# A two-block kernel on one core: first-norm statistics in the load stage, a bias read backwards, and first down weights split ahead

## The reference, cut to what matters

```
mod = silu(c) @ w_mod + b_mod;  sh1, sc1, g1, sh2, sc2, g2 = split(mod, 6)
h = rms(x, norm1_w) * (1 + sc1) + sh1
u, q, k, v = split(h @ w_in)             # 512, 512, 128, 128 columns
y_ssm  = z * sigmoid(z @ w_glu + b_glu), z = gelu(state space model of u)
y_attn = attention(rms(q), rms(k), v)    # window 128, logits + bias[bucket(distance)], a sink
x = x + g1 * (concat(rms(y_ssm), rms(y_attn)) @ w_out)
h2 = rms(x, norm2_w) * (1 + sc2) + sh2
val, gate = split(conv3(h2 @ w_up) + conv_b)
x = x + g2 * ((silu(gate) * val) @ w_down)         # inner width 2816
```

## Time and profile before

| | us |
|---|---|
| median of 3 executions (lowest, highest) | 2991.18 (2987.18, 2992.55) |
| the profiled execution, its own time | 2984.72 |
| its span, first to last instruction | 2982.9 |
| TensorE busy in the span | 2592.6 (87%) |
| VectorE busy | 1635.1 (55%) |
| ScalarE busy | 954.5 (32%) |
| mean granted TensorE clock | 0.931 of full |

### The profile page before, as it was taken

The page is one execution under the profiler, slowest core; times in us unless marked ns, Lnnn a source line. Parts: engine busy times, 40 slices in busy tenths (PEclk is TensorE's granted clock), DMA queues, the critical chain, the costliest instruction groups (busy, mean ns, idle before and its releaser), DMA issues. The chain is left out here.

```text
span 2982.9 us, 39459 instructions
## 1 busy us (share of the span) xinstructions
PE 2592.6 (87%) x16795; PEld 1389.9 (47%) x16795; DVE 1635.1 (55%) x2092; ACT 954.5 (32%) x1082; POOL 35.6 (1%) x66
## 2 busy tenths in 40 slices
PE   5988585899999989998785878897887999998997
PEld 2446463344444434443453657576332444443443
DVE  4767744654454443435205766668566677775243
ACT  3315204542332321313015454444343222222131
POOL 0010000010000000000000000000000000000000
PEclk7999798899999999999877989998999999999999
DMA  7125364212212113322010000000210112122433
GB/s 262 50 64 185 100 214 142 57 29 56 56 42 56 53 51 108 96 67 78 4 36 22 13 24 22 15 15 1 71 29 15 53 45 56 42 56 63 125 98 95
DMA packets 299447, 198.99 MB, mean 67 GB/s; under 512 B 11281, under 2 KB 294063, under 8 KB 298800
## 3 DMA queue, kind: packets, MB, share of 16 engines
q1 hardware_dynamic: 298438, 196.70, 22.2%
q10 hardware_dynamic: 873, 0.32, 0.0%
HBM read 187.02 MB, written 9.45 MB: 66 GB/s over the span
## 5 line engine op out<-in xcount | busy, mean ns | idle before, releaser
L199 PE MATMUL ps<-hT,arena 128*128 128x512 bf16 (+1 forms) x6384 | 1389.0, 380 | 80.5 <-DVE arena L238 24.2
L199 PEld LDWEIGHTS ps<-hT,arena 128*128 128x128 bf16 x6384 | 626.7, 99 | 831.3 <-issue 62.1
L199 PE MATMUL ps<-arena 128*128 128x512 bf16 x2112 | 462.5, 382 | 28.1 <-DVE arena L1781 28.1
L199 PEld LDWEIGHTS ps<-arena 128*128 128x128 bf16 x2112 | 207.8, 98 | 281.5 <-issue 37.6
L2022 DVE SCALAR_TENSOR_TENSOR arena<-ps,vec,arena 128x945 f32<-128x945 f32 (+2 forms) x176 | 215.1, 1222 | 79.2 <-ACT arena L2008 59.8
L1989 DVE SCALAR_TENSOR_TENSOR arena<-ps,vec,arena 128x1023 f32<-128x1023 f32 (+1 forms) x88 | 106.7, 1275 | 185.0 <-ACT arena L1979 185.0
L1781 DVE TENSOR_TENSOR arena<-hT,arena 128x2816 bf16<-128x2816 f32 x32 | 98.9, 3092 | 147.0 <-ACT arena L1777 146.9
L2614 PE MATMUL ps<-arena 128*128 128x128 f32 x896 | 125.8, 301 | 55.6 <-DVE arena L2884 46.6
L1777 ACT ACTIVATE arena<-hT 128x2816 bf16<-128x2816 f32 x32 | 81.6, 2550 | 283.0 <-DMA hT<-w_down_dram 106.8
L2614 PEld LDWEIGHTS ps<-arena 128*128 128x128 f32 x896 | 119.5, 214 | 62.5 <-DVE arena L2884 49.5
L1936 DVE TENSOR_TENSOR arena<-hT,arena 128x2048 bf16<-128x2048 f32 x44 | 100.9, 2292 | 35.7 <-ACT arena L1903 35.7
(11 more groups left out here) (405 smaller groups left out, 2594.8 us busy)
## 6 DMA issues: line engine op xcount, KB each, us to landing
xT<-ada_w_dram SPq DMA_DIRECT2D x24, 1024.0 KB, 6.4
hT<-w_up_dram SPq DMA_DIRECT2D x44, 512.0 KB, 5.0
hT<-w_down_dram SPq DMA_DIRECT2D x32, 704.0 KB, 6.7
hT<-ffn_up_dram SPq DMA_DIRECT2D x44, 512.0 KB, 4.9
hT<-ffn_down_dram SPq DMA_DIRECT2D x32, 704.0 KB, 7.0
arena<-w_in_dram SPq DMA_DIRECT2D x35, 512.0 KB, 4.1
xT<-w_mod_dram SPq DMA_DIRECT2D x16, 1024.0 KB, 5.2
arena<-w_mod_dram SPq DMA_DIRECT2D x8, 1024.0 KB, 19.1
```

What stands on the lines that cost most here:

```text
L199: last = pe.matmul(out, lhs(a, kt), rhs(b, kt, i), start=start and kt == 0 and (a, b) == (0, 0), stop=stop and kt == n_k - 1 and (a, b) == ...
```

## The change

1. **Statistics early.** `norm1` is made in stage_load. ScalarE squares the tiles as they are copied; TensorE sums half 0 by eight products with ones into bank 6 (no additions), half 1 goes by VectorE's additions and one product as before; Ln and Exp of both halves follow in pairs (`act_roots`). stage_project starts with the scaling. The root sits in `masks`.
2. **Mirrored bias.** The rows are copied reversed, so the windows land with the right partition and reversed columns, straight in `bias`; attention reads them with step -1. The flip, its product and its copy leave. The three small products stand behind the first `exact_half`.
3. **Loads.** The first three exact weights are loaded in stage_load; in stage_project the save of x, the other weights and two of the stream are issued ahead of the bias's round trip.
4. **x back.** Its load moves from the end of stage_ssm into stage_glu, behind two weights.
5. **First down weights.** Unit 0's are loaded once the last up weights are split and split in three pieces: rows 0 to 15, 16 to 20, and the last row at a place of its own. Even units keep two regions, odd ones another. TensorE makes rows 0 to 20 of units 0 and 1, then the last row of both, whose g is finished last.
6. **Later sums.** The sum in unit 9 stands ahead of row 18.

```diff
@@ stage_load: sync, scalar, tensor, vector
+            sp.wait_ge(turned, n_units + 1)
+            for n in range(3):
+                weights, source = exact_weights(k, n)
+                sp.dma_start(weights, source).then_inc(k.exact_in[n], 16)
...
+            def squares(first, end):
+                for i, n, a, b, t in norm.steps()[first:end]:
+                    act.wait_ge(copied, i + 1)
+                    if i >= 4:
+                        act.wait_ge(square_used if i < KD + 4 else norm.used, i - 3)
+                    act.activation(norm.sq[:, i % 4, :], k.xT[:, t, a:b], ACT.Square).then_inc(norm.sqd, 1)
+            squares(0, KD)
             act.wait_ge(copied, n_units + 2)
...
             act.activation(p_exp, p_exp, ACT.Exp).then_inc(exped, 1)
+            squares(KD, 2 * KD)
+            norm.act_roots(act)
...
+            pe.wait_ge(copied, n_units - 3)
+            square_sums(range(0, 4))
             pe.wait_ge(rows_in, 16 * len(loads))
...
             last.then_inc(turned, 1)
+            square_sums(range(4, KD))
+            pe.sem_inc(norm.summed, 1)
             pe.wait_ge(silu_c, 1)
...
+                if i == 5:
+                    norm.pe_sums(pe, (1,))
...
+            dve.wait_ge(norm.summed, 1)
+            dve.sem_inc(norm.used, KD)
+            norm.dve_stats(dve, (1,))
@@ stage_project: sync, scalar, vector
+            sp.dma_start(k.x_kept, k.xT[:, :, :]).then_inc(k.x_saved, 16)
...
-                        window = bass.AP(k.rows_dram, (4 * g + 2 * t + j) * RB, [[1, P], [1, 2 * WINDOW]])
-                        sp.dma_start(mirrored[:, 4 * g + 2 * j + t, :], window).then_inc(fetched, 16)
+                        window = bass.AP(k.rows_dram, (4 * g + 2 * t + j) * RB + 1, [[1, P], [1, 2 * WINDOW]])
+                        sp.dma_start(bias[:, 4 * g + 2 * j + t, :], window).then_inc(fetched, 16)
...
-            norm.act_squares(act)
-            norm.act_finish(act)
+            norm.act_affine(act)
...
-            norm.dve_centre(dve)
+            norm.dve_gain(dve)
+            norm.dve_finish(dve)
...
-            dve.tensor_copy(rows[0:N_Q, :], k.ps[0:N_Q, 6, 0:RB]).then_inc(copied, 1)
+            dve.tensor_copy(rows[0:N_Q, :], k.ps[0:N_Q, 7, P:P + RB][:, ::-1]).then_inc(copied, 1)
@@ stage_attention, stage_ssm, stage_glu
-                link(dve.scalar_tensor_tensor(x, src, scale, bias[:, g, :, 2 * WINDOW - nk:2 * WINDOW], ALU.mult, ALU.add))
+                link(dve.scalar_tensor_tensor(x, src, scale, bias[:, g, :, 0:nk][:, :, ::-1], ALU.mult, ALU.add))
...
-            sp.wait_ge(w_ready, 1)
-            sp.dma_start(k.xT[:, :, :], k.x_kept).then_inc(k.x_back, 16)
...
                 stream.load(sp, n)
+                if n == 1:
+                    sp.dma_start(k.xT[:, :, :], k.x_kept).then_inc(k.x_back, 16)
@@ DownByHalves, Ffn
+    def first_hi(self, act, f):
+        act.wait_ge(self.first_loaded, 32)
+        act.wait_ge(f.made[0], FT // 2 + 1)
+        for i, (raw, parts) in enumerate(self.first_splits()):
+            if i == 1:
+                act.wait_ge(f.done[0], FT // 2 + 1)
+            act.activation(parts[:, 0], raw, ACT.Copy).then_inc(self.first_hi_done, 1)
...
+    def first_units(self, pe, f):
+        pe.wait_ge(self.first_lo_done, 1)
+        self.span(pe, 0, 0, self.FIRST)
+        pe.wait_ge(self.first_lo_done, 2)
+        self.span(pe, 0, self.FIRST, FT - 1).then_inc(self.rows_done, 1)
+        pe.wait_ge(self.lo, 1)
+        self.span(pe, 1, 0, FT - 1)
+        pe.wait_ge(self.first_lo_done, 3)
+        pe.wait_ge(f.done[1], FT // 2 + 1)
+        for u in range(2):
+            self.span(pe, u, FT - 1, FT).then_inc(self.made, 1)
...
+        sp.wait_ge(self.lo[1], FT // 2 + 1)
+        down.load_first(sp)
         for b in range(2):
             sp.wait_ge(self.made[b], FT // 2 + 1)
...
         self.act_unit(act, FT // 2 - 1, 0)
-        self.act_unit(act, FT // 2 - 1, 1, down_hi)
+        down.first_hi(act, self)
+        self.act_unit(act, FT // 2 - 1, 1, lambda: down.split_hi(act, 1))
...
-                    if u == KD + 1 and kt == 6:
+                    if u == KD + 1 and kt == 18:
                         m_norm.pe_sums(pe, (0,))
```

More of the change, by code:

```diff
@@ L279, in stage_load @@
     p_exp, p_sum = (k.ar(M_BLOCKS + 2 * KD * 32 + 2 * HG_HEADS * i, 2 * HG_HEADS) for i in range(2))
+    k.norm1 = norm = norm1(k)
+    square_used = k.sem("square_used")
+    k.exact_in = [k.sem(f"exact_in{n}") for n in range(QK_TILES)]
     x_in = [k.sem(f"x_in{g}") for g in range(2)]
@@ L1781, in split_lo, with part @@
-        dve.tensor_tensor(self.parts(u, 1), self.raw, self.parts(u, 0), ALU.subtract).then_inc(self.lo, 1)
+        dve.wait_ge(self.hi, u)
+        for raw, parts in self.splits(u):
+            last = dve.tensor_tensor(parts[1], raw, parts[0], ALU.subtract)
+        last.then_inc(self.lo, 1)
+    def part(self, u, s, kt):
+        if u % 2:
+            return self.w_odd[:, s, kt, :]
+        if (u, kt) == (0, FT - 1):
+            return self.last_row[:, s, 0, :]
+        i = kt >= self.FIRST
+        return self.w_even[i][:, s, kt - self.FIRST * i, :]
@@ new lines, in span @@
+    def span(self, pe, u, first, end, before=None):
+        cols = slice((u // KD) * HALF, (u // KD + 1) * HALF)
+        for kt in range(first, end):
+            if before is not None:
+                before(kt)
+            for a, b in PASSES:
+                last = pe.matmul(self.bank(u), self.part(u, a, kt), self.g[:, b, kt, cols],
+                                 start=kt == 0 and (a, b) == (0, 0), stop=kt == FT - 1 and (a, b) == PASSES[-1],
+                                 skip_group_check=True)
+        return last
@@ L1785, in unit @@
[L1785 removed]
+        pe.wait_ge(self.lo, u)
         if u >= 4:
             pe.wait_ge(self.read, u + 1 - (4 if u < KD else self.second_banks))
[L1788 to L1790 removed]
+        self.span(pe, u, 0, FT, before).then_inc(self.made, 1)
     def bank(self, u):
@@ L2202, in _ @@
             act.wait_ge(ctx_saved, 16)
-            f.act(act, lambda: down.split_hi(act, 0))
-            act.wait_ge(f.done[0], FT // 2 + 1)
-            for u in range(1, 2 * KD):
+            f.act(act, down)
+            for u in range(2, 2 * KD):
                 down.split_hi(act, u)
@@ L3106, in turn @@
                 return last
-            for u in range(2 * KD):
+            down.first_units(pe, f)
+            for u in range(2, 2 * KD):
                 def before(kt):
-                    if u == 0:
-                        f.wait_last(pe, kt)
                     if KD <= u < KD + 4 and kt == 5:
```

211 lines of the change are left out of this document (119 added, 92 removed).

## The result

| | before | changed |
|---|---|---|
| median, us (lowest to highest, runs) | 2989.18 (2983.02 to 2992.55, 4) | 2911.36 (2909.44 to 2920.46, 4) |
| ratio, 95% interval | 1 | 0.9748 (0.9721 to 0.9775) |
| the profiled execution, us | 2984.72 | 2910.27 |
| mean granted TensorE clock | 0.931 | 0.945 |
| TensorE busy, us | 2592.6 | 2573.3 |

The account below looks back on a forecast made before the run. TensorE bounds the kernel; its holes and slow stretches behind them can be won. Gains 28.3 + 7.4 + 15.2 + 14.6 + 9.3 = 74.8 us from 2984.7 leave 2909.9; 6.5 carried over gives 2916 us, range 2905 to 2931.

Parts of the forecast that it names:

- the likeliest case: Whole kernel: the forecast itself, gains of 74.8 us giving 2916 us, held at 68% against four rivals.
- The start: Load stage to first exact product: early statistics and no flip start the first scaling 29.8 us earlier; gain 28.3 us.
- ScalarE is now the last: End of load stage: ScalarE's Ln, table load and two Exp finish last, at 39.0 us.
- The three small products: Projection: the bias's small products now stand between exact products and were charged 1.5 us.
- The mirrored bias: Attention: reading the bias backwards was taken to cost 0, with bounds 0 and 18.5 us.
- The gate: Gate's start: with two weights ahead of x, TensorE starts at 467.3 instead of 474.76; gain 7.4 us.
- The first down weights and the later sum: Down products: hole and slow unit go, 15.2 and 14.6 us; block 1's sum in unit 9 without wait, 9.3 us.
- The load stage: Rival, 12%: new sums run at TensorE's half level, the load stage ends some 6 us later; 2922 us.
- The weight chain: Rival, 14%: residuals come late in the down products, units cost 14.7 instead of 14.25 us; 2929 us.
- No part did nothing: Rival, 4%: early split held in a queue until the last up product, both blocks' 29.8 us stay; 2946 us.
- The backward read: Rival, 2%: attention's backward bias reads go element by element at eight times the time, adding 129 us; 3045 us.
- behind the first product the projection keeps its order: Projection: order kept and VectorE loses work, so the start's earlier shift goes through to the stage's end.

Follow-up runs that it names:

- old_sum: The changed kernel with the next norm's sum ahead of row 6 of unit 9 again; 2924.25 us, ratio 0.9780.
- old_start: The changed kernel with load and project stages and attention's bias read as before (parts 1, 2 and early exact weights undone); 2944.18 us, ratio 0.9848.
- changed_again: The changed kernel itself, unaltered, measured again on another chip beside the kernel before; 2916.24 us, ratio 0.9771.
- old_xback: The changed kernel with the load of x back at the end of the state space stage, ahead of the gate's weights; 2921.72 us, ratio 0.9778.
- negate_sum: The changed kernel with attention's negation of row maxima made as a SCALAR_TENSOR_TENSOR instead of a TENSOR_SCALAR; 2906.79 us, ratio 0.9730.
- old_down: The changed kernel with the first down weights loaded and split as before in both blocks (part 5 undone); 2943.90 us, ratio 0.9857.

## Why the prediction was right
**The range held and the likeliest case came**, 2916 against 2911.36, and 2916.24 for the changed kernel in its second measurement. The profiled execution took 2910.27 where the sum gave 2909.9; the 6.5 us carried over to the median were 1.1. Each of the gains came out within 2 us of what was worked out, but the near agreement of the total is partly luck: 5.8 us that the sum left out were lost, and 1.9 more than forecast at the start and 4.7 in stretches that nothing changed came back. Point by point:

*The start* (28.3, got 30.1). The working held at each end: the last modulation product at 37.9 and the first exact one at 41.7. "ScalarE is now the last" was wrong. The sum of half 1 was done at 33.8 and not 35.8. The transposes of x ended at 18.4 and not 19.4, and four sums of 0.92 us from 19.4 would end at 23.1, not at the 23.6 of the prediction. TensorE had no gap in which its clock fell, so the vectors took 0.70 and not 1.31 us, and five modulation products 4.50 and not 5.2. By 30.6 TensorE was through, and the sixth, with the sum behind it, waited only for its data at 31.70. The roots were ready at 37.0 and not 39.0, and VectorE's gain at 39.4 released the first scaling, at 39.45 where I had 39.8. The three small products, charged with 1.5 us, cost about that: the first six units and they take 87.08 - 41.72 = 45.36 us against 115.68 - 71.81 = 43.87, and the three by themselves 52.55 - 51.27 = 1.28. But the stage's last products made it good by 12.52 - 10.89 = 1.63 us, at a granted clock of 1.00 where it was 0.86, which I hadn't foreseen. That came in eleven of the twelve profiles with the early start; in old_sum they took 12.52 again.

*The mirrored bias* (0, bounds 0 to 18.5): 1225 ns before, after and read forward.

*The gate* (7.4, got 7.5): the wait went from 15.24 to 7.73.

*The first down weights and the later sum* (15.2 + 9.3 = 24.5 in block 1, got 57.3 - 33.2 = 24.1; 14.6 in block 2, got 74.3 - 60.7 = 13.6). The waits I had forecast in block 2 at 0.9 and 0.8 are there at 1.00 and 1.16. The sum has no wait, and unit 10's residual came 0.38 us late where I had 0.2.

*The rivals.* The load stage didn't grow: the granted clock from 20 us on is 1.00, where it was 0.67, as the sums fill that hole.

```profile
20.00:25.00 5.00, 5.00 (x17) 2.51 (x16) 1.75 (x6) 4.27 (x7) 0.00 (x0) 1.00 1.02 407
```

The weight chain doesn't run the down products: three waits of 2.5 us together. No part did nothing. The backward read isn't slower. The drain of 1.38 us that the Trainium skill ("ScalarE: Activation LUTs", What ACT_TABLE_LOAD costs) adds to each table load is again not in the rows: the table load at 34.55 begins 0.02 us after Ln ends and the Exp starts at its own end.

**What the sum left out.** It says "behind the first product the projection keeps its order ... so the shift goes through to the stage's end", which held to the end of that stage (30.2), and then takes the shift on to the gate. There two stages took 5.8 us: 2.6 in attention, where the hold is, and 3.2 in the state space stage. The size of the first is not shown to be the hold's: old_start, with the short holds, spent 105.6 us from attention's first product to the next stage's, and the nine profiles with the long hold 105.7 to 108.2 (changed_again has the 105.7), against 104.0 in the kernel before. What the runs show is that without any hold it is 96.2 to 96.4. The second loss is not settled. The stage's stretch, from its first product to the end of its last, in the kernel before, in the changed one and in old_start:

```profile
313.20:459.52 146.32, 105.25 (x2792) 82.89 (x2792) 87.31 (x138) 25.14 (x33) 3.52 (x1) 0.88 0.48 156
```
```profile
285.58:435.10 149.52, 107.20 (x2792) 84.73 (x2792) 87.36 (x138) 24.81 (x33) 3.51 (x1) 0.87 0.48 153
```
```profile
315.44:462.17 146.73, 104.94 (x2792) 83.39 (x2792) 87.29 (x138) 24.92 (x33) 3.52 (x1) 0.90 0.49 156
```

It takes 146.3 and 146.7 us in the two kernels with the late start and 147.8 to 150.9 in the twelve profiles with an earlier one, with the same instructions and nearly the same work on VectorE; the same kernel profiled twice has 149.5 and 148.8. It isn't the load of x back (149.8 in old_xback) nor the hold in attention (148.7 in negate_sum). The busy time of TensorE is 2.0 us higher in the changed kernel, at a clock of 0.87 against 0.88, but old_down has hardly more than before (105.5, at a clock of 0.90) and still takes 148.0. No run here was made to tell more.

Most of these 5.8 us was made good by chance. From the end of block 1's down product to the last up products of block 2 the change touches nothing, and that stretch took 1373.1 us before and 1369.8 in the profiled execution of the changed kernel; in the twelve other profiles it was 1367.8 to 1374.2, with 1374.0 in changed_again. So an estimate of what the change is worth, 74.3 less these 3.4, is 71 us, and the second measurement has 2985.90 - 2916.24 = 69.7.

## What to carry to other kernels
A hole of 7 to 15 us in TensorE cost its length here and then 1.7 to 2.8 us more at a lowered clock; both terms came out as read from the rows of before. When a shift is carried through a later stage, look there for instructions that take far longer than the others of their group, and not only for waits: this cost was already in the trace of before as a 128x4 instruction of 5.18 us, 32 times as long as the others, and no row showed it as idle time. In SyncE's queue the place of three loads of 0.5 MB behind or ahead of one of 4 MB was worth 10 us.

## What the runs showed of the hardware
A TENSOR_SCALAR of VectorE on SBUF (128x4, fp32) waited until GpSimd's MEMSET was through: 5.18 and 4.04 us in the kernel before, 12.09 us in the changed one, where it takes 0.16 us by itself. The profile counts the wait as the instruction's own duration. In the same place TENSOR_TENSOR and SCALAR_TENSOR_TENSOR with two inputs in SBUF took 0.15 to 0.16 us and RECIPROCAL 0.18 us under the memset, unheld (negate_sum's rows, while the first memset ran). The Trainium skill ("GPSIMD Engine Reference", Key points) says that GpSimd shares its SBUF interfaces with VectorE, with "contention with DVE instructions in a 2-port perf mode or with two SBUF inputs". The Trainium skill ("VectorE: DVE Perf Modes", Mode 2×_2P) says that such a mode reads one tensor in SBUF through both of VectorE's read ports, and that a fp32 tensor_scalar can run in it while a tensor_tensor can't. The trace agrees with the first half if this TENSOR_SCALAR ran in such a mode, which no row shows. It doesn't bear out the second half: the instructions with two SBUF inputs were not held by a MEMSET, the only kind of GpSimd instruction that ran there.

Whether VectorE got in between two memsets back to back varied between kernels; the one kernel with the hold that was profiled twice showed 12.09 us both times. In attention, a read with step -1 (128x1024, fp32) took 1.225 us, the same as forward.
